# A decoder layer on one core: the rounded dense weights over two buffers, an early expert slot, and a rearranged front, first and last quad

## The reference

```
mod   = silu(c) @ w_ada + b_ada                 # six vectors: sh1, sc1, gt1, sh2, sc2, gt2
h     = rmsnorm(x) * norm1 * (1 + sc1) + sh1
proj  = h @ w_in                                # attention q, k, v; mLSTM qk, v, o, gates; branch gates ga, gm
y_a   = differential attention (4 heads, ALiBi, causal)
y_m   = mLSTM (4 heads, causal convolution ahead of it)
x     = x + gt1 * ((sigmoid(ga) * (y_a @ w_br_a) + sigmoid(gm) * (y_m @ w_br_m)) @ w_out)
h2    = rmsnorm(x) * norm2 * (1 + sc2) + sh2
gate  = top-1 of 4 groups, top-2 of its 8 experts
x     = x + gt2 * sum over 32 experts of gate * (silu(h2 @ w1) * (h2 @ w3)) @ w2      # inner width 256
out   = rmsnorm(x) * norm_f
```

## Time and profile before

| | |
|---|---|
| median of 3 runs | 471.23 us |
| profiled execution | 471.42 us |
| its span, first to last instruction | 469.6 us |
| mean granted clock of TensorE | 0.954 |
| DMA, mean over the span | 350 GB/s |
| TensorE (PE) / VectorE (DVE) / ScalarE (ACT) / GpSimd (POOL) busy | 400.4 / 169.9 / 186.5 / 157.2 us |

### The profile page before, as it was taken

How to read it: one execution, slowest core, us unless ns; L and a number is a source line. 1 busy time by engine, 2 the same in 40 slices (tenths; PEclk the granted TensorE clock), 3 DMA queues, 4 the chain that set the end, 5 groups by cost and what they waited for, 6 DMA issues and landing times.

```text
span 469.6 us, 8607 instructions
## 1 busy us (share of the span) xinstructions
PE 400.4 (85%) x3612; PEld 309.5 (66%) x3612; DVE 169.9 (36%) x351; ACT 186.5 (40%) x343; POOL 157.2 (33%) x125
## 2 busy tenths in 40 slices
PE   6399999999799999999999889889897395682983
PEld 6299999888789999997986536355454162440541
DVE  1997166797027430475245130302111103011013
ACT  3577646663892394543354212131212011030122
POOL 0599776757448449996400000000000000000000
PEclk9799999999899999999999999899999689797798
DMA  8999997379979345749999879999999999999942
GB/s 338 423 416 427 416 421 304 125 264 395 424 305 411 116 158 180 269 180 391 422 421 376 361 287 423 421 419 420 421 420 421 423 421 419 421 419 422 421 182 91
DMA packets 23512, 164.30 MB, mean 350 GB/s; under 512 B 2608, under 2 KB 2736, under 8 KB 4656
## 3 DMA queue, kind: packets, MB, share of 16 engines
q1 hardware_dynamic: 23328, 163.20, 85.5%
q10 hardware_dynamic: 144, 0.52, 0.3%
HBM read 162.67 MB, written 1.05 MB: 349 GB/s over the span
## 4 chain that ended last, share of the span: by engine, by line
PE 68%; DMA 21%; DVE 5%; issue 2%; ACT 2%; SPq 2%; DVEq 0%
PE bank L1342 18%; DMA ring<-in_e 12%; PE cs_b L1342 9%; PE cs_b L1682 8%; DMA his<-in_e 6%; PE bank L1385 5%; PE bank L1648 5%; PE bank L1693 4%; PE bank L1637 3%; PE bank L1390 2%; PE cs_b L1295 2%; SPq L428 2%; DMA ring<-in_rest 1%; PE bank L1377 1%; PE cs_b L1637 1%
## 5 line engine op out<-in xcount | busy, mean ns | idle before, releaser
L501 POOL TENSOR_TENSOR ring_r<-ring,his_r 128x512 fp32r<-128x512 f32 x120 | 156.9, 1343 | 59.1 <-ACT his_r L524 59.1
L754 ACT ACTIVATE raw<-bank,sm 128x128 f32<-128x128 f32 x72 | 27.2, 458 | 151.1 <-PE bank L1648 151.1
L524 ACT ACTIVATE his_r<-ring 128x2048 fp32r<-128x2048 f32 (+1 forms) x32 | 57.6, 1800 | 27.0 <-DMA ring<-in_rest 13.5
L1682 PE MATMUL cs_b<-ring,raw 128*32 128x256 f32 x480 | 55.1, 397 | 7.3 <-DMA ring<-in_e 7.3
L1220 DVE TENSOR_TENSOR tmp<-cs_b,tmp 128x256 f32<-128x256 f32 x8 | 3.4, 424 | 134.3 <-ACT tmp L762 134.3
L1648 PEld LDWEIGHTS bank<-const,gm 128*128 128x128 f32 x288 | 34.1, 191 | 9.2 <-issue 6.7
L1682 PEld LDWEIGHTS cs_b<-ring,raw 128*32 128x32 f32 x480 | 27.6, 114 | 18.1 <-issue 11.6
L1648 PE MATMUL bank<-const,gm 128*128 128x128 f32 x288 | 35.8, 277 | 1.7 <-DVE const L1212 1.7
L1682 PE MATMUL cs_b<-his,raw 128*32 128x256 f32 x176 | 24.5, 398 | 8.0 <-DMA home<-in_e 8.0
L1682 PE MATMUL cs_b<-home,raw 128*32 128x256 f32 x112 | 23.5, 466 | 8.1 <-DMA ring<-in_e 8.1
L1342 PE MATMUL bank<-his_r 128*128 128x256 f32 x208 | 30.1, 288 | 0.0
(11 more groups left out here) (386 smaller groups left out, 813.9 us busy)
## 6 DMA issues: line engine op xcount, KB each, us to landing
ring<-in_e SPq DMA_DIRECT2D x47, 1024.0 KB, 26.1
ring<-in_rest SPq DMA_DIRECT2D x40, 1024.0 KB, 10.1
his<-in_e SPq DMA_DIRECT2D x16, 1024.0 KB, 23.8
home<-in_e SPq DMA_DIRECT2D x10, 1024.0 KB, 23.0
ring<-in_block SPq DMA_DIRECT2D x8, 768.0 KB, 20.1
o_att<-in_e SPq DMA_DIRECT2D x5, 1024.0 KB, 22.2
qkT<-in_e SPq DMA_DIRECT2D x5, 1024.0 KB, 25.8
mqk<-in_e SPq DMA_DIRECT2D x5, 1024.0 KB, 26.0
```

The costliest lines, as they stand in the source:

```text
L501: pool.tensor_tensor(ring_r[:, slot_of(n), sl], ring[:, slot_of(n), sl], hi(d)[:, sl].bitcast(F32), ALU.subtract).then_inc(s["w_lo"], 1)
L524: act.activation(hi(d)[:, 0:WIDTH[d]], ring[:, slot_of(n), 0:WIDTH[d]], ACT.Copy).then_inc(s["w_hi"], 1)
L754: ins = act.activation(xg[:, b, k, :], source[:, j * P:(j + 1) * P], ACT.Identity, bias=S("B2", KD)[:, k:k + 1], scale=S("A2", KD)[:, k:k ...
L1682: ins = pe.matmul(up_bank[e * CAP:(e + 1) * CAP, half], xg[:, b, k, e * CAP:(e + 1) * CAP], wt[e][:, k, :], start=(k == 0), stop=(k == KD ...
```

## The change

`HI` goes from 3 to 2: the rounded copies take turns in two buffers, and `split(d)` waits for unit d-2. The third buffer, which was also an expert slot, becomes one more part of `home` (`EXTRA`), used for an expert unit alone, and four expert units are loaded early, the first into it. At the front the first two slabs are normalized singly and the first modulation stands ahead of the sum of squares. The first quad multiplies by w3 right behind w1 and has no scatter; three small memsets stand for the large ones. The last quad has no gathers, no one-hot matrices and no gate transposes, and is written out behind the loop; the later passes build their first gathers themselves. The gate and rank tables lose their four extra columns. At the end ScalarE waits for each half of the output. Parts that only serve the later passes are left out below.

```diff
@@ -35,7 +35,7 @@
 LAMBDA_INIT = 0.8 - 0.6 * float(np.exp(-0.3 * 0))
 NEG = -1.0e30
 RING = 10
-HI = 3
+HI = 2
 SLOTS = RING + HI + 1
 UNIT = 2048
 PART = 512
@@ -85,7 +85,7 @@
 QUAD_UNITS = [(w, e) for w in ("w1", "w3", "w2") for e in range(QUAD)]
 UP_UNITS = 8
 QU = len(QUAD_UNITS)
-XSLOTS = SLOTS + 7
+XSLOTS = SLOTS + 8
 YSLOTS = 16
 LOOP = 4
 assert LOOP * QU % YSLOTS == 0 and NQ % LOOP == 0
@@ -109,7 +109,7 @@
     return RING + [UNIT_JOB[n] for n in DENSE].index(job) % HI
 
 
-HT, QKT, GM, MQK, LATE, X_HOME, XN_HOME, ATT = range(SLOTS, SLOTS + 8)
+HT, QKT, GM, MQK, LATE, X_HOME, XN_HOME, ATT, EXTRA = range(SLOTS, SLOTS + 9)
 MOD_HOME = (RING - 2, RING - 1, GM, MQK, X_HOME, XN_HOME, ATT, QKT)
 
 
@@ -122,12 +122,12 @@
 
 
 LAST = [place(n) for n in range(NPRE - RING, NPRE)]
-RELEASES = [(X_HOME, "mod"), (ATT, "mixed"), (XN_HOME, "aT3"), (LAST[0], "brm1"), (QKT, "brm3"), (LAST[1], "brm3")] + [(i, "ada5") for i in LAST[2:6]]
-RELEASES += [(MQK, "merged"), (LAST[6], "wo0"), (LAST[7], "wo1"), (hi_slot("wo1"), "wo1"), (LAST[8], "wo2"),
+RELEASES = [(EXTRA, None), (X_HOME, "mod"), (ATT, "mixed"), (XN_HOME, "aT3"), (LAST[0], "brm1"), (QKT, "brm3"), (LAST[1], "brm3")] + [(i, "ada5") for i in LAST[2:6]]
+RELEASES += [(MQK, "merged"), (LAST[6], "wo0"), (LAST[7], "wo1"), (LAST[8], "wo2"),
              (hi_slot("wo2"), "wo2"), (LAST[9], "wo3"), (hi_slot("wo3"), "wo3"), (SLOTS - 1, "wo3"),
              (HT, "lg"), (LATE, "x2n")]
 ORDER = [i for i, _ in RELEASES]
-EARLY = {NFIRST + 9: (0,), NFIRST + 21: (1,), NFIRST + 26: (2,)}
+EARLY = {NFIRST + 9: (0,), NFIRST + 10: (1,), NFIRST + 21: (2,), NFIRST + 26: (3,)}
 assert len(set(ORDER)) == XSLOTS
 
 BANK, TURN = {}, {}
@@ -538,7 +538,7 @@
                                bias=col("b_ada", k), scale=1.0)
                 link(act.activation(S("A1", KD)[:, k:k + 1], S("m1", 16)[:, 8 + k:9 + k], ACT.Identity,
                                     bias=S("nb", KD)[:, k:k + 1], scale=col("norm1", k)))
-                act.wait_ge(s["xn_r"], k // 2 + 1)
+                act.wait_ge(s["xn_r"], k + 1 if k < 2 else k // 2 + 2)
                 act.activation(hT_hi[:, k, :], hT[:, k, :], ACT.Identity, bias=S("B1", KD)[:, k:k + 1],
                                scale=S("A1", KD)[:, k:k + 1]).then_inc(s["h_hi"], 1)
                 if k >= 2:
@@ -755,31 +755,38 @@
                                          bias=S("B2", KD)[:, k:k + 1], scale=S("A2", KD)[:, k:k + 1])
                 ins.then_inc(s["g_evac"], 1)
 
-            def quad(it, b):
-                gather_half(1 - b, 0, it * 2 + 3)
-                gather_half(1 - b, 1, it * 2 + 4)
+            def quad(it, b, last=False):
+                if not last:
+                    gather_half(1 - b, 0, it * 2 + 3)
+                    gather_half(1 - b, 1, it * 2 + 4)
                 act.wait_ge(used, it * QU + UP_UNITS)
                 act.activation(sig, up_bank[:, 0:F], ACT.Sigmoid).then_inc(s["sig_r"], 1)
 
             gather_half(0, 0, 1)
             gather_half(0, 1, 2, pb("g1"))
-            with act.Fori(0, NQ // 2) as i:
+            with act.Fori(0, NQ // 2 - 1) as i:
                 for b in range(2):
                     quad(i * 2 + b, b)
+            quad(NQ - 2, 0)
+            quad(NQ - 1, 1, True)
             act.wait_ge(s["flag_r"], 1)
             over = act.value_load(flag[0:1, 0:1], min_val=0, max_val=1)
...
             act.activation(S("table", 1), ones[:, 0:1], ACT.Sqrt).then_inc(s["act_end"], 1)
 
 
             for tt in range(TT):
-                act.wait_ge(s["y_full"], tt + 1)
                 for c in range(2):
+                    act.wait_ge(s["y_full"], 2 * tt + c + 1)
                     act.activation(junk[:, (2 * tt + c) * 512:(2 * tt + c + 1) * 512], y_banks[2 * tt + c][:], ACT.Square,
                                    accum_out=S("ms5", 4)[:, 2 * tt + c:2 * tt + c + 1]).then_inc(s["sq5"], 1)
                 act.wait_ge(s["var5"], tt + 1)
@@ -846,8 +853,9 @@
 
             def normalize(i):
 
-                two = hT[:, 2 * i:2 * i + 2, :]
-                dve.tensor_tensor(two, two, r1b.unsqueeze(1).to_broadcast([P, 2, T]), ALU.mult).then_inc(s["xn_r"], 1)
+                some = hT[:, i:i + 1, :] if i < 2 else hT[:, 2 * i - 2:2 * i, :]
+                wide = r1b.unsqueeze(1).to_broadcast([P, 1 if i < 2 else 2, T])
+                dve.tensor_tensor(some, some, wide, ALU.mult).then_inc(s["xn_r"], 1)
 
             dve.wait_ge(const_in, 16)
             dve.tensor_scalar(S("dgain", 1), col("diff_norm"), 1.0 - LAMBDA_INIT, None, ALU.mult)
@@ -860,17 +868,17 @@
             dve.wait_ge(s["if_hi"], 1)
             dve.tensor_tensor(w_if_r[:, :, 8:16], K("w_if"), w_if_r[:, :, 0:8].bitcast(F32),
                               ALU.subtract).then_inc(s["if_hi"], 1)
+            dve.wait_ge(*full("cs0"))
+            dve.wait_ge(*full("cs1"))
+            modulation(0, 0)
+            modulation(0, 1)
             dve.wait_ge(*full("ss"))
             release(dve.tensor_scalar(r1b, pb("ss")[:, 0:T], 1.0 / D, EPS, ALU.mult, ALU.add), "ss")
             dve.wait_ge(s["std"], 1)
             link(dve.reciprocal(r1b, r1b))
             normalize(0)
-            dve.wait_ge(*full("cs0"))
-            dve.wait_ge(*full("cs1"))
-            modulation(0, 0)
-            modulation(0, 1)
             for k in range(KD):
-                if k < 3:
+                if k < 4:
                     normalize(k + 1)
                 if k < KD - 1:
                     modulation(k + 1, 0)
@@ -1109,9 +1117,8 @@
             for i in range(4):
                 residual(i)
 
-            dve.memset(ptg[:, 1], 0.0).then_inc(s["pt_evac"], 1)
-            dve.memset(outs2, 0.0).then_inc(s["o_dve"], 1)
-            dve.memset(hid, 0.0).then_inc(s["hid_done"], 1)
+            for i, name in enumerate(("pt_evac", "o_dve", "hid_done", "scat")):
+                dve.memset(S("idle", 4)[:, i:i + 1], 0.0).then_inc(s[name], 1)
 
             dve.wait_ge(s["sq2"], 1)
             link(dve.tensor_reduce(S("ms4s", TT), S("ms4", 8).rearrange("p (i t) -> p t i", t=TT), AX.X, ALU.add))
@@ -1163,8 +1170,7 @@
                                   ohg.unsqueeze(3).to_broadcast([P, TT, G, E]),
                                   m8.unsqueeze(2).to_broadcast([P, TT, G, E]), ALU.mult), "mask_r", 1)
 
-            NX = NE + QUAD
-            gate, rank = R("gate", TT, NX), R("rank", TT, NX)
+            gate, rank = R("g32", TT, NE), R("rank", TT, NE)
             dve.wait_ge(*full("rank"))
             link(dve.scalar_tensor_tensor(out=rank[:, :, 0:NE], in0=pb("rank")[:, 0:2 * NE].rearrange("p (t n) -> p t n", t=2),
                                           scalar=1.0, in1=mask, op0=ALU.add, op1=ALU.mult))
@@ -1175,8 +1181,6 @@
             dve.wait_ge(gt2_in, 16)
             spread(gt2b, 2, (0,))
             release(dve.reduce_max(S("cmax", 1)[0:1, :], pb("rank")[0:1, 2 * NE:3 * NE], AX.X), "rank")
-            link(dve.tensor_scalar(rank[:, :, NE:NX], rank[:, :, 0:QUAD], -float(CAP), None, ALU.add))
-
             dve.wait_ge(s["rexp"], 3)
             den = R("den", TT)
             link(dve.tensor_scalar(den, R("e2", TT), 1.0, None, ALU.add))
@@ -1192,8 +1196,6 @@
             link(dve.tensor_tensor(R("g32", TT, NE).rearrange("p t (g e) -> p t g e", g=G),
                                    ohg.unsqueeze(3).to_broadcast([P, TT, G, E]),
                                    we.unsqueeze(2).to_broadcast([P, TT, G, E]), ALU.mult))
-            link(dve.tensor_copy(gate[:, :, 0:NE], R("g32", TT, NE)))
-            link(dve.tensor_copy(gate[:, :, NE:NX], gate[:, :, 0:QUAD]))
             dve.wait_ge(s["moe_chain"], 1)
             dve.tensor_tensor(pgate[:], pone[:], gate[:, :, 0:QUAD].unsqueeze(3).to_broadcast([P, TT, QUAD, CAP]),
                               ALU.mult).then_inc(s["pg_ready"], 1)
@@ -1212,19 +1214,21 @@
                 dve.tensor_tensor(pgate[:], pone[:], gate[:, :, at].unsqueeze(3).to_broadcast([P, TT, QUAD, CAP]),
                                   ALU.mult).then_inc(s["pg_ready"], 1)
 
-            def quad(q, it, b):
-                dve.wait_ge(s["pt_full"], it + 1)
-                one_hot(bass.ds(q * QUAD + QUAD, QUAD), it * MC, 2)
+            def quad(q, it, b, turned, last=False):
+                if not last:
+                    dve.wait_ge(s["pt_full"], turned + 1)
+                    one_hot(bass.ds(q * QUAD + QUAD, QUAD), it * MC, 2)
 
                 dve.wait_ge(s["sig_r"], it + 1)
                 dve.tensor_tensor(act_a, up_bank[:, 0:F], sig, ALU.mult).then_inc(s["moe_chain"], 1)
-                dve.wait_ge(s["moe_chain"], it * MC + 3)
+                dve.wait_ge(s["moe_chain"], it * MC + (2 if last else 3))
                 dve.tensor_tensor(hid, up_bank[:, F:2 * F], act_a, ALU.mult).then_inc(s["hid_done"], 1)
 
-                dve.wait_ge(s["pt_full"], it + 2)
+                dve.wait_ge(s["pt_full"], turned + 2)
```

(49 more changed lines are left out.)

44 lines of the change are left out of this document (32 added, 12 removed).

## The result

The changed kernel takes **486.94 us** (median of 4, 485.53 to 488.35) against 470.96 for the kernel before beside it: ratio 1.033, 95% interval 1.028 to 1.039. It is slower by 16 us; I had forecast 479.7, 8.5 us over, with 486.0 as the upper end. The direction and the main term were right. The profiled execution took 486.21 (span 484.4), 14.8 more than the one of before.

What follows compares the result with a forecast made beforehand. TensorE's work bounds the dense stage, transfers the expert stage, so early delays count in full. -3.7 + 14.9 + 3.4 - 3.5 - 2.0 - 0.6 = +8.5 on 471.23 gave 479.7 us; range 473.5 to 486.0 (476 to 486: chance 0.70).

Steps and rivals of the forecast that it cites:

- Two buffers: Dense stage: with two rounded buffers for three, ScalarE's splits wait longer and hold work queued behind them; +14.9 us, bounds +8 and +18.
- (a): Split of ga2 waits for ga0's end, holding the attention-weight copies behind it: +2.7 us, of which 0.6 comes back.
- (b): Split of gm2 waits for gm0's end, so gm3 is split later and its low part comes late: +5.6 us.
- (c): Split of brm1 waits for bra1's end: low parts of y late by 0.9 us, low parts of w by 1.1.
- (d): Split of wo1 waits for brm3's end, holding the roundings of the merged branches: +5.6 us, less 0.4.
- Rival 1: Dense stage: the holds stay off the path and only the gains count, faster at 461.4 us; chance 0.06.
- Rival 2: Dense stage: an even bubble of 0.5 us per two units, some 3 us over twelve, 464.4 us; chance 0.05.
- rival 4: Whole kernel: holds lengthen each other and the clock stays low longer, beyond 486 us; chance 0.05.
- The clock: TensorE runs at a lowered clock after the new waits in gm3 and before wo0: +3.4 us, bounds 0 and 6.
- The first quad: First expert quad: w3 ahead of the gathers frees slots earlier and fills the DMA idle time: -3.5 us, bound -2.5.
- The front: Kernel start: modulation before normalizing and a single first slab let TensorE start at 16.35, not 20.00: -3.7 us.
- Last quad and end: Last expert quad without gathers and gate transposes, -2.0 us; at the end ScalarE squares each half earlier, -0.6 us.

## Why the prediction was right and where it was wrong

**What bounds the end** held: what is late before the first use of an expert unit arrives at the end in full. The two buffers alone show it with nothing else changed: 19.0 us there and 19.0 at the last landing.

**Two buffers: +14.9, measured 15.0 by the trace.** (a) ga1 starts 136.11, 2.5 later against ga0 than before, and 0.9 comes back by ga3: 1.7 (forecast 2.1, both with the part that comes back). (b) 7.6 us to the end of gm3, of which 1.85 is clock: 5.7 (5.6), with gm3's split at 179.90 where 181.1 + 2.1 less the front's 3.3 = 179.9 was due. (c) 2.5 (2.0), though on another path: I had 0.9 us of it on VectorE's low parts of y, which were in time (done at 205.8, and the job that reads them starts at 206.1); TensorE waits 0.24 and 1.48 us for GpSimd's low parts of the weights. (d) 5.1 (5.2). What made the sum right was one question for each split: what does it wait for now, and what is written behind it on the same queue. The moved splits show that this is the cause, since the same two buffers without the holds cost 17 us less. The Trainium skill (PSUM — Partial Sum Buffer, "Engine vs sequencer instructions") says that the queues of ScalarE, VectorE and GpSimd are strictly first in, first out. The trace agrees: the roundings at 221.36 start 0.09 us before the split ahead of them has ended, although their input was there before.

**Rival 1**, the holds off the path, fell. ScalarE was busy 40% and is busy 37%, and two buffers in its order cost 20 us, 17 of which a better order gives back. By the Trainium skill (Perfetto Trace Analysis, "Identifying the Most-Contended Engine") the engine of the highest occupancy is optimized first, and that is not ScalarE. Here the number that counts is not how busy an engine is but how long it works without a gap behind the wait: 10.9 us ahead of gm3's split. **Rival 2**, an even bubble, fell too: the loss is four single holds. The result lies in the range of **rival 4**, but the holds did not lengthen each other as it had it.

**The clock: +3.4, measured 4.6.** I priced two drops at 1.7 each from a row whose 0.64 over 4.7 us is 3.4 us of half clock. The two new drops lasted 6.83 us each: 1.85 in gm3, where TensorE was idle for part of it, and 2.71 at wo0, where it was busy for 6.14 of it. Here the mechanism was right and the size 1.2 us short.

**The first quad: -3.5, in the first profile +0.3.** This step failed, by 3.8 us, in one clause: "makes down start about 1 us later than now (an estimate); the transfers cover that". It starts 4.0 us later (24.15 against 20.19). 1.2 to 1.6 of that is the open evacuations and the sigmoid, near the estimate, as the kernels with full clock or nearly so show (21.35 to 21.8); the rest, 2.3 to 2.8, is half clock on gathers with waits around them. That dropping the scatter uncovered these waits is argued; that filling them gives the full clock back is shown. And the cover was thin: with 1 us of delay the issue behind the down part would have come 18.47 + 1 = 19.5 us after the first freed one, 0.5 us inside the edge of 20.0; it came after 24.15, 4.2 past it, which uses up the 3.9 us that the new order can give. I had priced the clock only in the dense stage. Over all runs the term is worth 1.2 (by the ratios, beside three buffers) to 3.7 us (by the medians, against the old quad put back), so the first profile shows less of it than the runs do. Its half clock is no rare case, though, as the trace with 22 extra matmuls and the one without the extra slot have 9.5 us of half clock there as well.

**The front: -3.7, measured -3.3** at the product that starts at 106.38 (before 109.70). TensorE starts 4.05 us earlier, and a low part of GpSimd is late in ml0 (the wait ends at 54.94). 0.4 more is gone when ga0 starts (122.19 for 125.09): the wait of 2.88 us before it goes back to the landing of a weight unit, which comes 3.1 us earlier (116.19 for 119.27), and the clock took the rest. Alone the front is worth 1.9 us by the ratio and 2.8 by its trace; beside three buffers the first freed issue came 0.2 us earlier in one trace and 2.8 in the other, with 6.83 us of half clock in the router stage and with 3.41.

**Last quad and end: -2.6, measured -2.2** in this profile (13.5 for 15.7). No run changed these alone. In the traces with the old last quad this part takes 14.3 to 15.7 us, in those with the new one 13.2 to 16.4, with means of 14.9 (3 traces) and 14.1 (15), so that the size of this term stays open between 0 and 2.5. The clock differs from trace to trace there too; that it causes the spread is argued.

**The miss, counted twice.** By the first profile: first quad 3.8, clock 1.2, front and the wait behind it 0.8, end 0.4, the holds 0.1, together the 6.3 us between 8.5 and 14.8. By the ratios of many runs: the two buffers with their clock cost 20.2 where I had 18.3, and all the rest gave 4.7 where I had 9.8, 7.0 us together. Of those 5.1 the front's share is 1.8 (1.9 for 3.7); how the other 3.3 divide between first quad, last quad and end is open, as the intervals are as wide as the terms. One cause is common to them: in the profiles it is the place of the half clock that decides whether such a gain arrives (shown within the first quad and at wo0, argued for the rest).

## What to carry to other kernels

Before taking a buffer away, list for each instruction that will wait longer what is written behind it on its engine, and follow that to who needs it; if it must wait, move the small urgent steps ahead of it: the same two buffers cost 20 us in one order and 3 to 7 in another ((0.9968 - 0.9901) x 471, and (0.9951 - 0.9810) x 471 with the sigmoid ahead in both). Price each new wait of TensorE twice, once for itself and once for the work behind it at half clock, and do so in every stage where cover is taken away. A gain that lies in keeping transfers going has an edge: work out how late the next issue may come before it is gone. And before a gain is put down to an edit, compare the stretches where the two kernels have the same code: of the 3.4 us that seemed the sigmoid's, 2.5 lay there.

## What the runs showed of the hardware

- Matmuls of 128x256 on rounded operands, 44 in a row, took 0.12 us each (5.45 us); one of plain float32 showed as two instructions of 0.22 us (14 in 3.19 us). I had taken 0.24 for both, so one filling was half as long as meant and one twice.
- With the wait ahead of wo0 cut from 6.06 to 3.31 us TensorE's clock still fell to 0.50; cut to 0.77 us it stayed at 1.00.
- The table load takes 1.28 us (from 291.38), and the sigmoid starts 0.01 us behind its end (292.67).
- The same kernel, profiled twice, had a mean granted clock of 0.73 and 0.87 from the first freed issue to the one behind the down part, which took 24.15 and 21.81 us.
